# Decode query copies and two layer-norm roots moved between prompt groups, one activation block ahead of the masked maximum, the last three key pages issued behind the value copy

## The chip, the cores and the metric

The kernel runs on one core of one Trainium2 chip. The time is the device time of one execution in microseconds; for the kernel before it is 1846.37 us, the median of three runs (1846.24 to 1847.13).

## The reference

One inference step of a hybrid decoder of two layers, in float32. A prompt of 512 tokens and eight decode sequences of 8 new tokens each (behind 2048 cached tokens) go through every layer. What bears on the change is the attention half of a layer:

```python
# prompt: per group g of 4 and block t of 128 queries
s = q @ k.T * scale                     # causal, selected and window branch
p = exp(where(mask, s, -1e30) - max); p /= sum(p)
o = gate_c * p_c @ v_cmp + gate_s * p_s @ v_sel + gate_w * p_w @ v_win
# decode: per sequence, 16 gathered pages of 128 keys
kcmp = rms_norm(gelu(blocks(keys) @ w1) @ w2);  vcmp = gelu(blocks(values) @ w1) @ w2
s = q @ k_sel.T * scale                 # over the 2048 gathered keys
# beside it: a convolution branch with a layer norm over 512 channels
c = silu((y - mean) * rsqrt(var + eps) * g + b)
x = x + concat(o, c) @ w_out;  x = x + ConvFFN(rms_norm(x))
```

## The kernel before, in words

Each engine has its own instruction stream, written out by hand, and engines wait for one another on counting semaphores (`wait_ge`). Nothing is scheduled by a tool: the order in the source is the order on the engine. Per layer the stages are `glu`, `project`, `compress`, `prompt`, `decode`, `mix`, `expand`, `contract`.

**compress.** The decode keys and values are folded into blocks by two-layer perceptrons. TensorE's `hidden` (L769) writes the first layer to PSUM; VectorE's `gelu_in` (L1815 to L1817) adds the bias and forms the argument of the tanh, and counts in `cmp_in`; ScalarE's `tanhed` and VectorE's `gelu_out` (L1852) finish it. At the end of this stage VectorE runs `cmp_max` (L1869 to L1875), `key_norm`, `ln_var` and one `gelu_in`.

**prompt.** Sixteen steps v, four groups by four query blocks; the blocks are taken in the order 1, 3, 0, 2, so a score tile is 256, 512, 128 or 384 wide. In step v, TensorE does `scores(v + 2)` (L836), `weigh(v - 1)` (L873, L876) and `turn(v)` (transposes, L855; for wide blocks also `lay`, some `hidden` matmuls). VectorE does `mask(v + 1)` (mask and maximum, L1927, L1930) and `weight(v)` (L1937 to L1943). ScalarE does the exponentials (L1409) and copies the transposes out of PSUM (L1272). All scores go to the same four banks, so `scores(m)` waits for `mask(m - 1)`. Between steps VectorE does other work: `gelu_in(1)`, the decode queries copied to QB and QD (L1959, L1965), the two reciprocals of the layer norm `ln_root` (L1803), its four `ln_scale` (L1807 to L1809), and two `gelu_out`.

**decode.** Four pairs p of sequences. A pair begins with `ks_in` (L914): TensorE waits until all 32 key pages of the pair, 16 for either sequence, have landed (64 KB each), and then makes the scores (L922). The pages of the first sequence are issued by SyncE, those of the second by ScalarE, in four portions between its own work in the pair before: pages 0 to 3, 4 to 9, 10 to 12 and 13 to 15. The last lines of TensorE in a pair are `weigh` (L1040), `values_second` (L709), `keys_T` (L756), some `hidden` or output matmuls, and a transpose of the pair's output (L1075), which waits for VectorE (L2068). ScalarE takes the result of `values_second` with `values_kept(bb)` (L1272, a count in `vct_kept`), that of `keys_T` with `keys_kept(bb)`, and then copies the transposed output (`s_kept`); TensorE waits for both counts in the next pair.

```python
pe.wait_ge(*count("ks_in", 512))                    # L914
```

Of the kernel before, what the change touches and what calls it, by code (L numbers as in the profile page):

```python
# [150 lines left out]
def build(nc, I, O):  # L151
    ctx = ExitStack()
    with ctx:
# [432 lines left out]
        def _(pe):  # L586
# [232 lines left out]
            def prompt(l):  # L819
                laid = [0]  # L820

                def lay(steps):
                    job, b, n, c, bank = late[0]
                    hidden(l, job, b, n, js=range(laid[0], laid[0] + steps), bank=bank, taken=6)
                    laid[0] += steps

                def scores(v):
                    g, t = STEPS[v]
                    if v:
                        pe.wait_ge(*count("masked"))  # L830
                    n = (t + 1) * P
                    hp = [slice(HD * h, HD * (h + 1)) for h in range(2)]
                    q = [QT[hp[h], g, t * P:(t + 1) * P] for h in range(2)]
                    for e in range(2):
                        for h in range(2):
                            ins = mm(ps[:, 2 * e + h, 0:n], q[h], KT[hp[h], e, 0:n], start=True, stop=True)  # L836
                    ins.then_inc(sh["sc_made"], 1)

                def next_bank():
                    seen_of["pt_kept"] += 1  # L840
                    if seen_of["pt_kept"] > 2:
                        pe.wait_ge(sh["pt_kept"], seen_of["pt_kept"] - 2)
                    return 7 - seen_of["pt_kept"] % 2

                def turn(v):
                    t, pb = STEPS[v][1], PB[v % 3]
                    pe.wait_ge(*count("p_ready"))
                    for h in range(2):
                        if v == 0 and h == 1:
                            pe.wait_ge(*count("ct_kept", 2))  # L850
                        tiles = [(e, k) for e in range(2) for k in range(t + 1)]
                        for i in range(0, len(tiles), 4):
                            bank = next_bank()
                            for j, (e, k) in enumerate(tiles[i:i + 4]):
                                ins = tr(ps[:, bank, j * P:(j + 1) * P], pb[2 * h + e][:, k * P:(k + 1) * P], ident[:, :])  # L855
                            ins.then_inc(sh["pt_made"], 1)
                        if t >= 2 and h == 0:
                            lay(1 if v in (1, 13, 15) else 2)

                def weigh(v):  # L860
                    g, t = STEPS[v]
                    if v >= 13:
                        lay(1)
                    pe.wait_ge(sh["pt_kept"], seen_of["pt_kept"])
                    if v:
                        pe.wait_ge(*count("o_kept"))
                    out = [ps[HD * h:HD * (h + 1), 5, 0:P] for h in range(2)]
                    for e in range(2):
                        for k in range(t + 1):
                            j = e * (t + 1) + k  # L870
                            for h in range(2):
                                c = KVB + (3 + 2 * e) * P + HD * h
                                mm(out[h], Z[:, k, c:c + HD], PT[2 * h + j // 4][:, j % 4, :], start=j == 0, stop=False)  # L873
                    for h in range(2):
                        r = 32 * (2 * (g % 2) + h)
                        ins = mm(out[h], Vc[4][r:r + NCP, HD * h:HD * (h + 1)], CT8[r:r + NCP, 2 * t + g // 2, :], start=False, stop=True)  # L876
                    ins.then_inc(sh["o_made"], 1)

                pe.wait_ge(*count("cs_max"))
                pe.wait_ge(sh["var_made"], 6 * l + 4)  # L880
                scores(0)
                pe.wait_ge(sh["cmp_in"], 16 * l + 5)
                hidden(l, 2, 3, 1, js=range(8), bank=4)
                scores(1)
                hidden(l, 2, 3, 1, js=range(8, 16), bank=4)
                pe.wait_ge(sh["vct_kept"], NJOB * l + 3)
                cmp_turned()
                pe.wait_ge(sh["kct_kept"], NJOB * l + 3)
                scores(2)
                pe.wait_ge(sh["cmp_in"], 16 * l + 6)  # L890
                turn(0)
                for v in range(1, 16):
                    if v < 14:
                        scores(v + 2)
                    weigh(v - 1)
                    turn(v)
                weigh(15)
                pe.wait_ge(*count("masked"))
                pe.wait_ge(*count("o_kept"))
# [367 lines left out]
        def _(act):  # L1267
# [179 lines left out]
            def decode(l):  # L1447
                for p in range(NPR):
# [14 lines left out]
                    def fetch_keys(gs):  # L1463
                        for g in gs:
                            act.dma_start(ksT[1][:, P * g:P * (g + 1)],  # L1465
                                          I["ksT"][l, ds(page[g], 1)].rearrange("a p e -> (a p) e")).then_inc(sh["ks_in"], 16)
# [36 lines left out]
                    if more:  # L1503
                        ba, bb = JOBS[p][0][0], JOBS[p][1][0]
                        keys_squared(NCS)
                        values_kept(NCS, Vc[ba % 4], 2)
                        tanhed(tanh[1 if p < 2 else 2], NCS)
                        fetch_keys(range(10, 13))
                        keys_kept(NCS, KcT[ba % 4])
                        fetch_keys(range(13, 16))  # L1510
                        keys_squared(NCS)
                        values_kept(NCS, Vc[bb % 4], 3)
                        keys_kept(NCS, KcT[bb % 4])
                    act.wait_ge(*count("ot_made"))
                    for h in range(2):
# [104 lines left out]
        def _(dve):  # L1620
# [268 lines left out]
            def compress(l):  # L1889
                dve.wait_ge(*count("posb_kept"))  # L1890
                gelu_in(0, NCS, 2)
                taps(3, 10, 18)
                dve.wait_ge(*count("posb_kept"))
                gelu_in(1, NCS, 2)
                gelu_out(0, NCS, 2)
                gelu_out(1, NCS, 2)
                taps(3, 18, 26)
                gelu_in(0, NCM, 0, 5)
                key_means(NCS)
                taps(3, 26, 30)  # L1900
                key_norm(NCS)
                gelu_out(0, NCM, 0)
                taps(3, 30, CW)
                gelu_in(1, NCM, 0, 7)
                channel_sums()
                key_means(NCP)
                gelu_out(1, NCM, 0)
                key_norm(NCP)
                ln_centre()
                key_means(NCS)  # L1910
                cmp_max()
                key_norm(NCS)
                ln_var()
                gelu_in(0, NCS, 0)

            def prompt(l):

# [27 lines left out]

                if l:
                    dve.wait_ge(sh["causal_in"], 16 * l)
                mask(0)
                cmp_weight()
                mask(1)  # L1950
                weight(0)
                gelu_in(1, NCS, 0, 4)
                if l:
                    dve.wait_ge(sh["s_kept"], l * NPR)
                dve.wait_ge(*count("tr_kept", 10))
                for h in range(2):
                    hp = slice(HD * h, HD * (h + 1))
                    for g in range(G):
                        ins = dve.tensor_copy(QB[hp, :, 32 * h + 8 * g:32 * h + 8 * g + 8],  # L1959
                                              QT[hp, g, SEQ:NT].rearrange("p (b i) -> p b i", b=DB))  # L1960
                step(ins)
                for h in range(2):
                    src = QB[HD * h:HD * (h + 1), :, 32 * h:32 * (h + 1)]
                    for r in range(2):
                        ins = dve.tensor_copy(QD[HD * r:HD * (r + 1), :, 32 * h:32 * (h + 1)], src)  # L1965
                ins.then_inc(sh["qb_made"], 1)
                for v in range(1, 16):
                    if v < 15:
                        mask(v + 1)
                    weight(v)  # L1970
                    if v in (1, 4):
                        ln_root(v // 4)
                    if v == 6:
                        gelu_out(0, NCS, 0)
                        gelu_out(1, NCS, 0)
                    if v in (5, 8, 9, 12):
                        ln_scale((5, 8, 9, 12).index(v))
                count("pt_made", sum(BANKS[t] for g, t in STEPS[13:]))
                weight_sums_of(1)
                dve.wait_ge(sh["uc_out"], 16 * (l + 1))  # L1980
# [381 lines left out]
```

## Time and profile before

| | |
|---|---|
| median of 3 runs | 1846.37 us |
| profiled execution, own time | 1854.27 us |
| its span in the trace | 1852.5 us |
| TensorE matmuls, busy | 1816.2 us, 98% |
| VectorE busy | 1240.4 us, 67% |
| ScalarE busy | 381.3 us, 21% |
| mean granted TensorE clock | 0.994 |

The span is one profiled execution; the profile's times are microseconds from its start. PE is the matmul stream, PEld its weight loads, DVE is VectorE, ACT ScalarE, POOL GpSimd; SPq and ACTq are the sequencers of SyncE and ScalarE, which issue transfers. A row of the timeline gives start, duration, engine, line, operation, output and inputs, the count of merged instructions, and in brackets the idle time before it with what ended that. The granted clock is the share of 2.4 GHz: 1.00 is 2.4 GHz and 0.50 is 1.2 GHz.

The prompt stage of layer 0 stands at 215 to 304 us, its decode at 304 to 430; those of layer 1 at 1134 to 1223 and 1223 to 1350.

### The profile page before, as it was taken

What the parts mean: (1) busy time and instruction counts of PE and PEld (TensorE: products, weight loads), DVE (VectorE), ACT (ScalarE), POOL (GpSimd) and SP (SyncE); (2) the same over time, 40 slices, a digit from 0 to 9 for tenths busy, and PEclk for the clock granted to TensorE, in tenths of its full rate; (3) what the DMA queues carried; (4) which work ended last, traced back from release to release, by engine and by line L of the source; (5) the groups of instructions that cost most, each with busy time, mean ns of one, the idle gap of its engine ahead of it and who ended that gap; (6) DMA issues with size and microseconds to landing.
All of it is one profiled execution on the core that took longest, in us unless ns stands there. A gap on an engine that the chain in (4) does not pass through costs nothing.

```text
span 1852.5 us, 28010 instructions
## 1 busy us (share of the span) xinstructions
PE 1816.2 (98%) x10702; PEld 1406.2 (76%) x10702; DVE 1240.4 (67%) x2742; ACT 381.3 (21%) x993; POOL 118.9 (6%) x218
## 2 busy tenths in 40 slices
PE   9999999999999999999999999999999999999999
PEld 7767677787777777777777676778777777777777
DVE  5899897562676776663268997966527677676631
ACT  2013375332101000100001124853221100000000
POOL 1011400110000000000000114000100000000000
PEclk9999999999999999999999998999999999999999
DMA  7302554763122121221241044057431212222111
GB/s 279 130 1 79 169 199 144 243 210 142 46 80 80 69 91 68 78 118 63 100 153 60 1 137 130 2 179 245 172 123 49 88 68 91 68 79 111 63 63 52
DMA packets 110536, 200.15 MB, mean 108 GB/s; under 512 B 13409, under 2 KB 81266, under 8 KB 105410
## 3 DMA queue, kind: packets, MB, share of 16 engines
q1 hardware_dynamic: 91090, 162.13, 25.9%
q0 software_dynamic: 5488, 29.93, 4.6%
q10 hardware_dynamic: 13824, 6.30, 1.2%
q8 instruction: 85, 1.39, 0.3%
q14 instruction: 49, 0.40, 0.1%
HBM read 190.62 MB, written 15.94 MB: 112 GB/s over the span
## 4 chain that ended last, share of the span: by engine, by line
PE 92%; DVE 4%; issue 1%; ACT 1%; ACTq 1%; DMA 0%; POOL 0%; SPq 0%; DVEq 0%
PE ps L1106 31%; PE ps L1171 15%; PE ps L631 9%; PE ps L666 8%; PE ps L618 7%; PE ps L769 5%; PE ps L962 5%; PE ps L873 2%; PE ps L836 2%; PE ps L855 2%; PE ps L907 1%; PE ps L1040 1%; PE ps L674 1%; PE ps L922 1%; ACTq L1465 1%
## 5 line engine op out<-in xcount | busy, mean ns | idle before, releaser
L2238 DVE TENSOR_TENSOR xT<-xT,ps 128x288 f32<-128x288 f32 (+3 forms) x55 | 41.7, 758 | 153.2 <-PE ps L1171 152.6
L1106 PE MATMUL ps<-catT,rD 128*128 128x288 f32 x528 | 131.6, 406 | 0.0
L1550 ACT ACTIVATE rD<-rD 128x592 f32<-128x592 f32 x44 | 30.7, 698 | 450.0 <-DVE rD L2180 450.0
L1106 PEld LDWEIGHTS ps<-catT,rD 128*128 128x128 f32 x528 | 100.3, 190 | 27.7
L1106 PE MATMUL ps<-catT,XC 128*128 128x288 f32 x480 | 119.8, 406 | 0.4 <-DVE rD L2152 0.4
L1106 PE MATMUL ps<-rA,WR 128*128 128x288 f32 x448 | 117.8, 406 | 0.0
L1106 PEld LDWEIGHTS ps<-catT,XC 128*128 128x128 f32 x480 | 91.0, 190 | 26.2 <-issue 1.2
L1272 ACT ACTIVATE rC<-ps 128x256 f32<-128x256 f32 (+8 forms) x162 | 58.2, 387 | 232.9 <-PE ps L666 118.8
L631 PE MATMUL ps<-catT,WR 128*128 128x288 f32 x384 | 99.9, 413 | 4.4 <-issue 2.4
L1106 PEld LDWEIGHTS ps<-rA,WR 128*128 128x128 f32 x448 | 85.1, 190 | 23.5
L618 PE MATMUL ps<-rA,WR 128*128 128x288 f32 x384 | 93.4, 406 | 0.0
L1106 PE MATMUL ps<-rA,rB 128*128 128x288 f32 x336 | 88.5, 407 | 2.8 <-DVEq L2175 2.8
L631 PEld LDWEIGHTS ps<-catT,WR 128*128 128x128 f32 x384 | 71.8, 192 | 24.8 <-issue 4.8
L1691 DVE SCALAR_TENSOR_TENSOR catT<-XC,par,catT 128x512 f32<-128x512 f32 x120 | 89.6, 747 | 0.0
L618 PEld LDWEIGHTS ps<-rA,WR 128*128 128x128 f32 x384 | 73.0, 190 | 20.2
L1691 DVE SCALAR_TENSOR_TENSOR YB<-XC,par,YB 128x512 f32<-128x512 f32 x112 | 83.6, 747 | 0.0
L1106 PEld LDWEIGHTS ps<-rA,rB 128*128 128x128 f32 x336 | 63.7, 190 | 21.1 <-DVEq L2175 3.7
L666 PE MATMUL ps<-rB,rA 128*128 128x326 f32 x256 | 71.6, 437 | 0.0
L2144 DVE TENSOR_TENSOR rD<-rD,ps 128x288 f32<-128x288 f32 x42 | 19.1, 454 | 78.3 <-PE ps L1106 78.3
L666 PEld LDWEIGHTS ps<-rB,rA 128*128 128x128 f32 x256 | 48.5, 189 | 21.7
L769 PE MATMUL ps<-WR,rD 128*128 128x258 f32 (+1 forms) x256 | 59.8, 384 | 0.2
L1106 PE MATMUL ps<-catT,WR 128*128 128x288 f32 x224 | 58.9, 406 | 0.0
(405 smaller groups left out, 3527.6 us busy)
## 6 DMA issues: line engine op xcount, KB each, us to landing
WR<-in_w_up SPq DMA_DIRECT2D x56, 512.0 KB, 3.7
WR<-in_kvc SPq DMA_DIRECT2D x128, 128.0 KB
rB<-in_w_up SPq DMA_DIRECT2D x32, 512.0 KB, 4.4
rD<-in_kvc SPq DMA_DIRECT2D x96, 128.0 KB, 2.5
rD<-in_w_down SPq DMA_DIRECT2D x8, 1408.0 KB, 7.7
rB<-in_ksT SPq DMA_DIRECT2D x160, 64.0 KB
rB<-in_w_down SPq DMA_DIRECT2D x6, 1408.0 KB, 7.8
WR<-in_w_glu SPq DMA_DIRECT2D x16, 512.0 KB, 4.0
```

What stands on the lines that cost most here:

```text
L618: ins = mm(ps[:, bank + hf, 0:HN], w[:, k * P:(k + 1) * P], rhs[:, k, hf * HN:(hf + 1) * HN], start=k == 0, stop=k == K - 1)
L631: ins = mm(ps[:, bank, 0:HN], w[:, k, :], rhs[:, k, hf * HN:(hf + 1) * HN], start=k == first, stop=k == last)
L666: ins = mm(ps[0:m, 4 * (t % 2) + ch, 0:CHW], hT[:, k, t * P:t * P + m], weights(ch, k), start=k == 0, stop=k == KD - 1)
L769: ins = mm(out[:, 0:2 * nb].rearrange("p (c h) -> p c h", h=2), w1[n][:, j, :], chunks[:, j // NPAIR:j // NPAIR + nb, o:o + 2], start=j == ...
L836: ins = mm(ps[:, 2 * e + h, 0:n], q[h], KT[hp[h], e, 0:n], start=True, stop=True)
L855: ins = tr(ps[:, bank, j * P:(j + 1) * P], pb[2 * h + e][:, k * P:(k + 1) * P], ident[:, :])
L962: ins = mm(thirds(bank)[part], w, rows[:, :, o:o + 2], start=j == 0, stop=j == NPAIR - 1)
L1106: ins = mm(ps[:, bank, 0:HN], w[:, k, :], h[:, k, :], start=k == 0, stop=k == 3)
L1171: ins = mm(ps[:, bank, 0:HN], w(k), h(k), start=k == 0, stop=k == FH - 1)
L1272: return act.activation(out, in_, ACT.Copy)
L1691: ins = stt(y, xc[:, k:k + SEQ], w, y, ALU.mult, ALU.add)
L2238: step(tt(x, x, src, ALU.add))
```

## The change: what it does

Four edits, without any instruction added or taken out but one wait:

1. TensorE's wait for the sixth count of `cmp_in` ahead of `turn(0)` is gone. The first `lay`, in `turn(1)`, waits for the same count already.
2. In `compress` VectorE's `gelu_in(0)` stands ahead of `cmp_max` and not behind `ln_var`.
3. In `prompt` VectorE's `gelu_in(1)` moves from ahead of step 1 to between `mask(2)` and `weight(1)`; the query copies move to step 8; the two `ln_root` from steps 1 and 4 to 4 and 6; the four `ln_scale` from 5, 8, 9, 12 to 9, 10, 12, 13.
4. In `decode` ScalarE issues pages 13 to 15 behind `keys_squared` and `values_kept(bb)` and not ahead of them.

```diff
@@ compress and prompt, TensorE @@
                 scores(2)
-                pe.wait_ge(sh["cmp_in"], 16 * l + 6)
                 turn(0)
@@ decode, ScalarE @@
                         fetch_keys(range(10, 13))
                         keys_kept(NCS, KcT[ba % 4])
-                        fetch_keys(range(13, 16))
                         keys_squared(NCS)
                         values_kept(NCS, Vc[bb % 4], 3)
+                        fetch_keys(range(13, 16))
                         keys_kept(NCS, KcT[bb % 4])
@@ compress, VectorE @@
                 key_means(NCS)
+                gelu_in(0, NCS, 0)
                 cmp_max()
                 key_norm(NCS)
                 ln_var()
-                gelu_in(0, NCS, 0)
@@ prompt, VectorE @@
+                def queries_laid():
+                    if l:
+                        dve.wait_ge(sh["s_kept"], l * NPR)
+                    dve.wait_ge(*count("tr_kept", 10))
...
+                    ins.then_inc(sh["qb_made"], 1)
+
                 mask(0)
                 cmp_weight()
                 mask(1)
                 weight(0)
-                gelu_in(1, NCS, 0, 4)
-                if l:
-                    dve.wait_ge(sh["s_kept"], l * NPR)
-                dve.wait_ge(*count("tr_kept", 10))
...
-                ins.then_inc(sh["qb_made"], 1)
                 for v in range(1, 16):
                     if v < 15:
                         mask(v + 1)
+                    if v == 1:
+                        gelu_in(1, NCS, 0, 4)
                     weight(v)
-                    if v in (1, 4):
-                        ln_root(v // 4)
+                    if v in (4, 6):
+                        ln_root(v // 6)
+                    if v == 8:
+                        queries_laid()
                     if v == 6:
                         gelu_out(0, NCS, 0)
                         gelu_out(1, NCS, 0)
-                    if v in (5, 8, 9, 12):
-                        ln_scale((5, 8, 9, 12).index(v))
+                    if v in (9, 10, 12, 13):
+                        ln_scale((9, 10, 12, 13).index(v))
```

The body of `queries_laid` is the code that stood in line before. Line numbers of VectorE's part are one to five lower after the change.

VectorE at the start of the prompt stage, before the change: the end of `weight(0)`, then `gelu_in(1)`, the query copies, and the first instruction of `mask(2)`.

```order
L1943 TENSOR_SCALAR rA<-rA,st 128x256 x4
L1815 TENSOR_SCALAR rC<-ps,posb 128x254
L1816 SCALAR_TENSOR_TENSOR rC<-rC 128x254
L1817 SCALAR_TENSOR_TENSOR rC<-rC 128x254
L1959 COPY QB<-rC 64x8x8 x8
L1965 COPY QD<-QB 64x8x32 x4
L1927 ISA XC,st<-ps,causal 128x128
```

And the same place with the change:

```order
L1942 TENSOR_SCALAR rA<-rA,st 128x256 x4
L1926 ISA XC,st<-ps,causal 128x128
...
L1929 TENSOR_SCALAR st<-st 128x4
L1814 TENSOR_SCALAR rC<-ps,posb 128x254
L1815 SCALAR_TENSOR_TENSOR rC<-rC 128x254
L1816 SCALAR_TENSOR_TENSOR rC<-rC 128x254
L1936 TENSOR_SCALAR st<-st 128x4
```

`mask(2)` follows `weight(0)` at once, and `gelu_in(1)` stands behind it.

VectorE at the end of step 8 with the change: the end of `weight(8)`, the query copies, and the first instruction of `mask(10)`. Before, the three instructions of an `ln_scale` stood in the place of the copies.

```order
L1942 TENSOR_SCALAR XC<-XC,st 128x256 x4
L1954 COPY QB<-rC 64x8x8 x8
L1960 COPY QD<-QB 64x8x32 x4
L1926 ISA rC,st<-ps,causal 128x128
L1926 ISA st 128x1
```

ScalarE near the end of a pair in decode, before the change; a DMA row is one key page, and `kct_made` and `cmp_out` are counts by TensorE of a transpose and of a second layer.

```order
L1272 ACTIVATE rC<-ps 128x127 [waits kct_made]
L1465 ISA
L1465 DMA rB<-in_ksT 128x128
...
L1465 DMA rB<-in_ksT 128x128
L1350 ACTIVATE KN<-ps 127x128 [waits cmp_out]
L1272 ACTIVATE rC<-ps 127x128 [waits cmp_out]
```

With the change:

```order
L1271 ACTIVATE rC<-ps 128x127 [waits kct_made]
L1349 ACTIVATE KN<-ps 127x128 [waits cmp_out]
L1271 ACTIVATE rC<-ps 127x128 [waits cmp_out]
L1464 ISA
L1464 DMA rB<-in_ksT 128x128
L1464 ISA
L1464 DMA rB<-in_ksT 128x128
L1464 ISA
L1464 DMA rB<-in_ksT 128x128
```

The three pages now stand behind the second `cmp_out`, which TensorE counts after its last weighted sums of the pair.

## Rows read from the trace of the kernel before

**Rows 1.** The page, part 1: TensorE's busy time and share.

```profile
PE 1816.2 (98%) x10702; PEld 1406.2 (76%) x10702; DVE 1240.4 (67%) x2742; ACT 381.3 (21%) x993; POOL 118.9 (6%) x218
```

**Rows 2.** Timeline, TensorE, layer 0 prompt: scores and weighted sums, steps 1 and 5.

```profile
231.69 2.12 PE L836 MATMUL ps<-rC 64*128 64x384 f32 x8 [1.70 <-DVE st L1930]
233.74 1.98 PE L873 MATMUL ps<-rA,rC 128*64 128x128 f32 x16
...
252.00 1.56 PE L836 MATMUL ps<-rC 64*128 64x384 f32 x8 [0.59 <-DVE st L1930]
253.49 1.09 PE L873 MATMUL ps<-rA,rC 128*64 128x128 f32 x16
```

**Rows 3.** Timeline, VectorE, same stretch: gelu_in(1), the query copies, ln_root(0).

```profile
226.92 0.48 DVE L1815 TENSOR_SCALAR rC<-ps,posb 128x254 f32<-128x254 f32 x1
...
228.23 1.01 DVE L1959 COPY QB<-rC 64x64 f32<-64x64 f32 x8
229.27 1.19 DVE L1965 COPY QD<-QB 64x256 f32<-64x256 f32 x4
...
233.74 1.94 DVE L1803 RECIPROCAL rA<-rA 128x288 f32<-128x288 f32 x1
```

**Rows 4.** Timeline, TensorE, layer 1 prompt: scores of step 1.

```profile
1150.04 2.29 PE L836 MATMUL ps<-rC 64*128 64x384 f32 x8 [1.70 <-DVE st L1930]
```

**Rows 5.** Windows: stretch, length, busy PE PEld DVE ACT POOL, granted clock, DMA share, GB/s.

```profile
229.10:232.50 3.40, 1.47 (x10) 0.97 (x12) 3.15 (x19) 2.09 (x8) 1.70 (x3) 1.00 1.45 431
232.50:235.90 3.40, 3.40 (x24) 1.99 (x22) 3.37 (x6) 0.82 (x5) 0.00 (x0) 0.51 0.81 325
362.30:365.70 3.40, 2.05 (x59) 1.63 (x58) 1.34 (x6) 0.28 (x1) 0.70 (x1) 1.00 1.04 313
365.70:369.10 3.40, 3.40 (x32) 1.75 (x39) 1.12 (x5) 1.43 (x6) 0.00 (x0) 0.50 0.59 192
```

**Rows 6.** Timeline, steps 8 and 11 of layer 0: last mask instruction, TensorE's next scores.

```profile
270.23 0.17 DVE L1930 TENSOR_SCALAR st<-st 128x4 f32<-128x4 f32 x1
270.45 1.56 PE L836 MATMUL ps<-rC 64*128 64x384 f32 x8
278.94 0.17 DVE L1930 TENSOR_SCALAR st<-st 128x4 f32<-128x4 f32 x1
280.10 1.99 PE L836 MATMUL ps<-rC 64*128 64x512 f32 x8
```

**Rows 7.** Timeline, ScalarE, end of pair 0, layer 0: page issues, keys squared, values_kept(bb).

```profile
330.41 1.82 ACTq L1465 DMA_DIRECT2D rB<-in_ksT  x3
332.28 0.28 ACT L1350 ACTIVATE KN<-ps 127x128 f32<-127x128 f32 x1 [1.72 <-PE ps L709]
333.85 0.28 ACT L1272 ACTIVATE rC<-ps 127x128 f32<-127x128 f32 x1 [1.29 <-PE ps L709]
```

**Rows 8.** Timeline, TensorE, end of pair 0: keys_T, and the next pair's scores.

```profile
334.57 0.33 PE L756 MATMUL ps<-ident,KN 127*128 127x127 f32 x1 [0.75 <-DVE KN L1863]
...
335.63 1.95 PE L922 MATMUL ps<-rB,QD 64*32 64x512 f32 x32
```

**Rows 9.** Timeline, pair 2 of layer 0, and a window (columns as in rows 5).

```profile
396.03 1.49 ACTq L1465 DMA_DIRECT2D rB<-in_ksT  x3
399.47 0.28 ACT L1272 ACTIVATE rC<-ps 127x128 f32<-127x128 f32 x1 [1.63 <-PE ps L709]
400.91 1.95 PE L922 MATMUL ps<-rB,QD 64*32 64x512 f32 x32
398.50:399.00 0.50, 0.50 (x16) 0.41 (x11) 0.00 (x0) 0.00 (x0) 0.50 (x1) 1.00 0.05 11
```

**Rows 10.** Timeline, pair 1: SyncE's transfers in layer 0, the rest in layer 1.

```profile
358.96 10.94 SPq L359 DMA_DIRECT2D rD<-in_kvc  x16
1280.12 1.35 ACTq L1465 DMA_DIRECT2D rB<-in_ksT  x3
1284.19 0.45 ACT L1272 ACTIVATE rC<-ps 127x128 f32<-127x128 f32 x2 [2.39 <-PE ps L709]
1285.09 0.18 PEld L922 LDWEIGHTS ps<-rB,QD 64*32 64x32 f32 x16 [0.31 <-DMA rB<-in_ksT]
```

More of the change, by code:

```diff
@@ L1947, in prompt @@
                     dve.wait_ge(sh["causal_in"], 16 * l)
+                def queries_laid():
+                    if l:
+                        dve.wait_ge(sh["s_kept"], l * NPR)
+                    dve.wait_ge(*count("tr_kept", 10))
+                    for h in range(2):
+                        hp = slice(HD * h, HD * (h + 1))
+                        for g in range(G):
+                            ins = dve.tensor_copy(QB[hp, :, 32 * h + 8 * g:32 * h + 8 * g + 8],
+                                                  QT[hp, g, SEQ:NT].rearrange("p (b i) -> p b i", b=DB))
+                    step(ins)
+                    for h in range(2):
+                        src = QB[HD * h:HD * (h + 1), :, 32 * h:32 * (h + 1)]
+                        for r in range(2):
+                            ins = dve.tensor_copy(QD[HD * r:HD * (r + 1), :, 32 * h:32 * (h + 1)], src)
+                    ins.then_inc(sh["qb_made"], 1)
                 mask(0)
@@ L1951, in prompt @@
                 weight(0)
-                gelu_in(1, NCS, 0, 4)
-                if l:
-                    dve.wait_ge(sh["s_kept"], l * NPR)
-                dve.wait_ge(*count("tr_kept", 10))
[L1956 to L1965, printed above, removed]
-                ins.then_inc(sh["qb_made"], 1)
                 for v in range(1, 16):
```

## Prediction

> **What bounds the kernel now.** I read the page first: TensorE is busy for 98% of the span [rows 1]. So an edit gains only where it shortens a wait of TensorE or raises its clock, and costs only where it makes TensorE wait or lowers its clock. I then read TensorE's timeline for its idle time in the two stages that the change touches, the windows for the clock granted there, and the timelines of VectorE and ScalarE for what stood ahead of the instruction that ended each wait.
>
> In the prompt stage one wait stands out. The scores of step 1 start after 1.70 us of idle time, ended by VectorE's last mask instruction [rows 2]; in layer 1 it is 1.70 us again [rows 4]. VectorE had reached that mask late: ahead of it stood gelu_in(1), from 226.92, and the query copies, from 228.23 to 230.46 [rows 3]. None of them is needed by these scores.
>
> Right behind this wait the granted clock falls: TensorE is busy for 1.47 of 3.40 us, and in the next 3.40 us it has 0.51 of the full clock, that is its lower level, 1.2 GHz [rows 5]. The scores take 2.12 us where the same shape takes 1.56, and the weighted sums 1.98 where they take 1.09 [rows 2].
>
> In decode I looked at how a pair hands over to the next. ScalarE issues the last three key pages of pair 0 at 330.41; the copy behind which the change puts them starts at 333.85 [rows 7]. TensorE starts the next pair at 335.63 [rows 8], and it may not start before the last page is there. For pair 1 of layer 1 it even waits for the page already, 0.31 us, though the issue was at 1280.12 and the start at 1285.09 [rows 10]. That is the place which decides.
>
> **The change part by part.**
>
> *The missing wait of TensorE and gelu_in(1) behind mask(2).* With gelu_in(1) and the copies gone from its way, VectorE has mask(2) ready about 2.7 us sooner, before TensorE's transposes end. The 1.70 us go in each layer. The transposes themselves gain nothing from the missing wait: their second half waits for a copy of ScalarE. Since TensorE is then busy through this stretch, I expect the lower clock to go with the wait: (2.12 - 1.56) + (1.98 - 1.09) = 1.45 us, about 1.6 with the shorter pieces behind. The bounds are 0, if the clock falls all the same, and 1.7, half of 3.4 us. Together -3.3 us per layer.
>
> *What the moved VectorE work then costs.* A piece of work between steps is free only as far as VectorE is ahead of TensorE. At step 8 the mask ends at 270.40 and TensorE takes up its scores at 270.45 [rows 6]: there is no room, and the ln_scale that stood there (1.35 us) is replaced by the copies, 1.01 + 1.19 us plus gaps, 2.27 [rows 3]. That makes a new wait of 0.9 - 0.1 = 0.8 us. At step 10 an ln_scale comes in where the mask had 280.10 - 279.11 = 1.0 us to spare [rows 6]: 1.35 - 1.0, about 0.4. At step 6 a root of 1.94 us [rows 3] comes in and an ln_scale goes at step 5: between 0 and 0.6, I take 0.3. Step 4 keeps a root as before, with its wait of 0.59 [rows 2]. Step 13 and the missing root of step 1 lie beside idle time of VectorE. Given back: 1.5 us per layer. Query copies are needed only by decode, so step 8 is early enough; SyncE waits for them behind the end of the prompt stage, so nothing in its queue gets later.
>
> *gelu_in(0) ahead of cmp_max.* It moves into idle time of VectorE, while the scores which were its cover keep running; TensorE's next matmuls wait 0.1 us less. Prompt stage: -3.3 + 1.5 - 0.1 = -1.9 us per layer, **-3.8 us** in all.
>
> *The last three pages.* ScalarE works in order, so they are issued 0.1 us after values_kept(bb) starts. What lies between the first issue and the last landing? In pair 2 of layer 0 the issue is at 396.03 and the transfers have ended in the window that begins at 398.50, some 2.9 us later [rows 9]: this is the lower bound. The upper bound is from pair 1: at most 4.97 us in layer 1 [rows 10], with SyncE's 16 transfers of 10.94 us running beside it [rows 10]. So for pair 0 of layer 0: 333.85 + 0.1 + 2.9 = 336.9 against 335.63, a loss of 1.3 us. Pair 2: 399.47 + 3.0 = 402.5 against 400.91, 1.6 us. Layer 1 has the same pattern: 1.45 and 1.7. For pair 1 the lower bound gives 1284.19 + 3.0 - 1285.09 = 2.1 us and the upper one 4.2; in layer 0 it is 1.5 to 4.6. I take 4.8 us for the two: SyncE's queue is behind there, so when TensorE comes later, SyncE's transfers end sooner beside it. Sum of the six: 1.3 + 1.6 + 1.45 + 1.7 + 4.8 = **+10.9 us**, bounds 9.7 and 14.9.
>
> There is a gain in this edit, but it is swallowed. The squaring at 332.28 came after the issues [rows 7]; without them keys_T would lose its wait of 0.75 us [rows 8]. TensorE only comes to the page wait sooner. What stands behind the three issues on ScalarE gets late too: keys_kept(bb) and the copy of the pair's output, which TensorE needs for the second half of the key scores. At 336.8 it is there just before the pages, so it is hidden by them, and would cost 0.4 us per pair if they were not late.
>
> *The clock in decode.* TensorE stands still for about 2 us at five of the six hand-overs at least, and the work before it is made of small matmuls. In layer 0 a stretch of this kind, 2.05 us busy out of 3.40, is already followed by 3.4 us at 0.50 [rows 5]. I reckon with such a fall at five of the six, each at the 1.6 us of the prompt stage, less the one that is there now: 5 x 1.6 - 1.6 = **+6.4 us**. The bounds are -1.6 (none, and the present one gone) and 8.6 (six, at 1.7).
>
> **The sum** is -3.8 + 10.9 + 6.4 = +13.5 us. The durations are from an execution of 1854.27 us (span 1852.5), which is 7.9 us over the median; I carry the difference over: 1846.37 + 13.5 = 1859.9 us.
>
> **The rivals.**
>
> *Waits without the clock.* The pages are late as above, but the clock holds or falls no more often than now: -3.8 + 10.9 = +7.1, 1853.5 us. For it: pair 0 has idle pieces in decode now without a fall at the hand-over. Against it: those are below 1 us.
>
> *Every hand-over falls to the low clock, and pair 1 waits its upper bound.* After each late page the first 3.4 us run at half speed: -3.8 + 14.9 + 8.0 = +19.1, 1865.5 us. For it: the fall at 365.70 came with 2.05 us of work in the stretch before [rows 5], and the new gaps leave less. Against it: SyncE's queue drains sooner. The Trainium skill, "TensorE: Matmul & The Clock Gate", section "HAM oscillation — how this bites in real kernels", describes exactly this: a kernel that waits for a transfer ahead of each tile loses the clock ahead of each tile, and pays every time. By that rule this rival would be the result; the trace agrees as far as the fall behind the 1.70 us wait of both prompt stages goes.
>
> *The pages come in time.* If ScalarE's queue ran ahead of its waiting copy, or three pages landed within 1.1 us (the time from values_second to the next pair without the keys_T wait), only the prompt gain would remain, less 0.3 us per pair for the output copy: -3.8 + 1.8 = -2, 1844.4 us, not slower. It decides at a loss of about 0.6 us per pair. Against it: the three issues alone take 1.35 to 1.82 us [rows 7, 10], and they are seen behind a waiting copy, never ahead of it.
>
> *The change doesn't do what it says in the prompt.* The clock falls there all the same, or the new waits of steps 6, 8 and 10 take everything: -3.8 becomes 0, 1863.7 us.
>
> **How the numbers follow.** Forecast 0.48; waits without the clock 0.17; every hand-over and the upper bound 0.17; no prompt gain 0.11; pages in time 0.04; something in my reading of decode that I don't see, on either side, 0.03. The likeliest case gives 1859.9. The range takes in the first three and the fourth with their bounds: 1852 to 1867. A measurement of this kernel can tell about 0.2%, 3.7 us, from no change. Slower by more than that holds in all cases but the pages in time and part of the unseen: 0.93. Same 0.04, faster 0.03.
>
> **What the new profile would show.** Right in the prompt: the scores of step 1 start without idle time, full clock behind them, a wait of some 0.8 us at the scores after step 8. Right in decode: PEld L922 of pairs 1 to 3 waits for DMA rB<-in_ksT, 2 us and more, the three ACTq rows start 0.1 us after values_kept(bb), and stretches of 0.50 clock follow. I am wrong if the L922 rows show no DMA wait, or if TensorE's later waits in a pair shrink by as much as the page wait adds.

## The result and the profile after

The changed kernel takes 1876.86 us (median of 4 runs, 1871.82 to 1881.51) against 1846.30 us before, measured beside it: ratio 1.015, 95% interval 1.0128 to 1.0171 (the quotient of the two medians, 1.0166, lies inside it). The forecast was 1859.9 us, with a range of 1852 to 1867. The direction was right and the size was not: +30.6 us, where +13.5 was expected. The time lies above the range and above the slowest rival, 1865.5 us.

The profiled execution took 1876.91 us with a span of 1874.8 us, so it stands for the median. The one before took 7.9 us more than its median. Part of that can be seen: in its compression stage of layer 1 TensorE ran 10.2 us at the lower clock, which the profile after does not have. The stage took 62.07 us there and 57.29 us after, 4.78 us that no edit made; four of the experiments below show the same piece in layer 0.

The page of the changed kernel, part 1 [rows 1]:

```profile
PE 1814.8 (97%) x10702; PEld 1399.3 (75%) x10702; DVE 1240.5 (66%) x2742; ACT 379.6 (20%) x993; POOL 118.3 (6%) x218
```

TensorE's timeline: layer 0's prompt stage, steps 1, 5, 7, 9 and 11, then four of the six hand-overs in decode [rows 2, 8 to 10]:

```profile
229.03 0.66 PE L855 MATMUL ps<-ident,rA 128*128 128x128 f32 x4 [1.00 <-ACT rB L1271]
229.62 1.56 PE L836 MATMUL ps<-rC 64*128 64x384 f32 x8
231.12 1.09 PE L873 MATMUL ps<-rA,rC 128*64 128x128 f32 x16
...
248.35 1.56 PE L836 MATMUL ps<-rC 64*128 64x384 f32 x8 [0.59 <-DVE st L1929]
258.27 1.99 PE L836 MATMUL ps<-rC 64*128 64x512 f32 x8 [0.29 <-DVE st L1929]
268.07 1.56 PE L836 MATMUL ps<-rC 64*128 64x384 f32 x8 [0.87 <-DVE st L1929]
278.05 1.99 PE L836 MATMUL ps<-rC 64*128 64x512 f32 x8 [0.34 <-DVE st L1929]
...
335.18 3.67 PE L921 MATMUL ps<-rB,QD 64*32 64x512 f32 x32 [3.50 <-DMA rB<-in_ksT]
373.43 3.67 PE L921 MATMUL ps<-rB,QD 64*32 64x512 f32 x32 [4.31 <-DMA rB<-in_ksT]
415.74 3.56 PE L921 MATMUL ps<-rB,QD 64*32 64x512 f32 x32 [8.23 <-DMA rB<-in_ksT]
...
1342.44 3.67 PE L921 MATMUL ps<-rB,QD 64*32 64x512 f32 x32 [5.79 <-DMA rB<-in_ksT]
```

The prompt stage came out as forecast. The scores of step 1 start without idle time and run at full clock (1.56 and 1.09 us, where they took 2.12 and 1.98). The new waits behind steps 6, 8 and 10 are 0.29, 0.87 and 0.34 us; I had written 0.3, 0.8 and 0.4. (The scores at 270.45 in [rows 6], headed step 8 there, are TensorE's step 9; the mask ahead of them follows VectorE's step 8.) From the stage's first scores to the first scores of decode it is 87.16 us where it was 89.08, and 87.17 for 89.09 in layer 1: -1.9 us per layer.

The loss is in decode. The group of the first key scores, by form, says how much TensorE waits for the last pages: 30.0 us, all at six hand-overs.

```profile
L921 PE MATMUL ps<-rB,QD 64*32 64x512 f32 x256 | 25.6, 932 | 30.9 <-DMA rB<-in_ksT 30.0 <-issue 0.8
```

The windows over the two decode stages split the loss. Columns as in [rows 5]; first the kernel before, then the changed one. Each stretch runs from the first key scores to the first product of the expansion, so the short `mix` stage is in it too.

```profile
304.74:489.88 185.14, 180.36 (x1905) 147.76 (x1906) 100.11 (x303) 50.95 (x128) 12.33 (x16) 0.99 0.56 185
1223.12:1411.43 188.31, 180.69 (x1906) 148.36 (x1906) 100.28 (x303) 50.92 (x128) 12.35 (x16) 0.99 0.55 177
```

```profile
302.68:506.64 203.96, 184.87 (x1905) 148.03 (x1906) 100.38 (x303) 50.55 (x128) 12.30 (x16) 0.93 0.51 168
1233.16:1433.75 200.59, 183.52 (x1906) 147.83 (x1907) 100.50 (x303) 50.55 (x128) 12.32 (x16) 0.96 0.50 166
```

Length less busy time of PE is its idle time. Both stages together grow from 373.45 to 404.55 us, by 31.1. Idle time grows from 12.4 to 36.2, by 23.8; busy time grows from 361.1 to 368.4, by 7.3, with the same instructions, so that is the lower clock (0.93 and 0.96 granted in place of 0.99). My terms for the two were +10.9 and +6.4. The account closes: 31.1 - 3.8 (prompt) - 4.8 (the piece that was chance) = 22.5 us, and the spans differ by 22.3.

So the clock's term was about right, and the pages' term was less than half of what came. Why are the pages that late? At the hand-over after pair 2 of layer 0, ScalarE and GpSimd of the changed kernel show this:

```profile
406.29 1.00 POOL L509 DMA_INDIRECT rC<-in_cache_v_slc,idx  x1 [0.61 <-PE ps L1039]
407.59 0.95 POOL L509 DMA_INDIRECT rC<-in_cache_v_slc,idx  x1 [0.30 <-issue]
...
406.63 0.28 ACT L1271 ACTIVATE rC<-ps 127x128 f32<-127x128 f32 x1 [2.24 <-PE ps L709]
406.76 1.80 ACTq L1464 DMA_DIRECT2D rB<-in_ksT  x3
```

and the DMA view of 406.7 to 416 us has these queues and issues:

```profile
q0 software_dynamic: 288, 2.10, 60.1%
q10 hardware_dynamic: 432, 0.20, 7.3%
...
rC<-in_cache_v_slc,idx POOLq DMA_INDIRECT x2, 7.0
```

From the first issue to the scores it is 415.74 - 406.76 = 9.0 us, for 0.2 MB. (In a second profile of the same kernel, which stands under "The clock's share" below, this hand-over took 6.5 us with a wait of 5.70, so 9.0 is the worst case seen and not the rule.) The same instruction that ends a pair's weighted sums (pv_done) releases GpSimd's two gathers for the pair after, 2.1 MB. Before the change the last pages were issued 3 us ahead of that point; now they are issued 0.5 us behind it. The trace of before had the row that I did not read, at 399.31, where values_kept(bb) starts at 399.47 [rows 9]:

```profile
399.31 1.00 POOL L509 DMA_INDIRECT rC<-in_cache_v_slc,idx  x1 [0.17 <-issue]
```

At pair 1 the gathers wait for something else, but there pv_done releases SyncE's window and new rows for pair 3. The changed kernel shows them beside the pages, which are issued at 367.85 and take 5.6 us from there to the scores: SyncE's timeline, and the DMA view of 366 to 374 us with the size and the time from issue to landing:

```profile
367.12 0.39 SPq L364 DMA_DIRECT2D rC<-in_kwT  x1
367.56 1.00 SPq L365 DMA_DIRECT2D rC<-in_state_v_win  x1
```

```profile
rC<-in_kwT SPq DMA_DIRECT2D x1, 512.0 KB, 3.5
rC<-in_state_v_win SPq DMA_DIRECT2D x1, 512.0 KB, 5.7
```

At pair 0 pv_done releases no transfer at once. That gave the theory for the experiments. **A:** pages 13 to 15 are late because they enter the DMA engines together with what pv_done releases. **B**, the rival: they are late by issue time and latency alone, and the traces of before were too few to show how long that is. A second question is how much of the loss is the clock, and a third whether the prompt edits have any part in the decode loss.

### The profile page after: what moved, and what is told of

The parts are those of the page before. It is cut to its first block, busy times and chain, and to the rows that moved or that the text cites. A ratio compares the mean times of both kernels' runs of the same rounds, so it can differ in the third digit from the quotient of the medians.

```text
span 1874.8 us, 28011 instructions
## 1 busy us (share of the span) xinstructions
PE 1814.8 (97%) x10702; PEld 1399.3 (75%) x10702; DVE 1240.5 (66%) x2742; ACT 379.6 (20%) x993; POOL 118.3 (6%) x218
## 4 chain that ended last, share of the span: by engine, by line
PE 89%; DVE 6%; DMA 2%; issue 1%; ACT 1%; ACTq 1%; DVEq 0%
PE ps L1105 30%; PE ps L1170 15%; PE ps L631 8%; PE ps L666 7%; PE ps L618 7%; PE ps L769 5%; PE ps L961 4%; PE ps L1039 2%; PE ps L836 1%; DMA rB<-in_ksT 1%; PE ps L921 1%; PE ps L873 1%; PE ps L906 1%; PE ps L855 1%; PE ps L674 1%
```

## Experiments

Ratios are to the kernel before, run on the same chip, with 95% intervals. Its medians there lie between 1847.9 and 1850.8 us, so ratios are compared and not medians.

### The pages back, and the pages alone

The changed kernel with the issues where they were:

```
-                        keys_squared(NCS)
-                        values_kept(NCS, Vc[bb % 4], 3)
                         fetch_keys(range(13, 16))
+                        keys_squared(NCS)
+                        values_kept(NCS, Vc[bb % 4], 3)
```

> The changed kernel with the last three key pages issued where they were before, ahead of keys_squared(bb); the prompt-stage edits stay. Theory A (the whole loss is in the decode hand-overs, the prompt edits gain 1.9 us per layer): no wait of PEld L921 for rB<-in_ksT over 0.4 us, and 3.8 us faster than before, 1842.5 us. Rival (the prompt edits disturb decode too, through the later query layout or a shifted clock): a time between 1846 and 1877.

Measured: 1845.11 us, ratio 0.998 (0.9967 to 0.9992), that is -3.7 us (0.002 x 1851). TensorE waits 1.3 us for pages in all, at one hand-over (pair 1 of layer 1, where the kernel before waited 0.31); theory A had no wait over 0.4, so on that point it missed. The two decode stretches take 371.66 us together, where the kernel before took 373.45.

The kernel before with the opposite edit and nothing else:

> The kernel before with nothing changed but the three issues moved behind values_kept(bb). Theory A: the six hand-overs cost 30.5 + 3.8 = about 34 us by themselves, 1880.5 us, with some 30 us of waiting for the pages as in the changed kernel. Rival B (the landing takes the 2.9 to 5 us that the trace of before shows, and the prompt edits made the rest of the loss): 17 us by my forecast's own terms, 1863.6 us.

Measured: 1875.42 us, ratio 1.0134 (1.0119 to 1.0149), +25 us, with 24.0 us of page waits. Theory A of that run had said 34 us; the waits were 6 us shorter than in the changed kernel. But 17 us, all that my forecast's terms give, is outside the interval too (1.0092). Together: the prompt edits gain 3.7 us and lose nothing in decode that these runs can show; the page edit makes the whole loss. The two do not add exactly (+25 - 3.7 is 21, the changed kernel has +28 by its ratio). Against the changed kernel's first profile the difference in the waits is all in layer 0. At pair 1 this run waits 2.42 us, and the changed kernel 4.31 and 4.13 in its two profiles. Here SyncE issues its window at 372.97, 1.9 us behind the pages (371.12); in the changed kernel it does so at 367.12, 0.7 us ahead of them. At pair 2 it is 5.17 against 8.23 and 5.70, so two profiles of one kernel differ there by as much.

### The collision taken away

SyncE and GpSimd wait until the next pair's pages have landed:

```
                     if p == 1:
+                        sp.wait_ge(sh["ks_in"], 512 * (NPR * l + 3))
                         fetch_window(l, 3)
...
                             pool.wait_ge(sh["imp_kept"], NPR * l + p + 2)
+                        else:
+                            pool.wait_ge(sh["ks_in"], 512 * (NPR * l + 4))
                         gather_values(l, p + 1)
```

> The changed kernel, with two groups of transfers held back until the next pair's key pages have landed: SyncE's window and new rows for pair 3 (released by pv_done of pair 1) and GpSimd's two gathers for pair 3 (released by pv_done of pair 2). Theory A (in pairs 1 and 2 the three pages share the DMA engines with 1.0 MB and 2.1 MB that pv_done releases at the same moment): the waits of the pairs 1 and 2 fall from 4.3, 8.2, 5.7 and 5.8 us to about the 2.5 to 3.5 us of the two pairs 0, some 10 to 12 us less in all, 1865 to 1867 us. Rival B (issue time and the latency of one transfer are all): the waits stay, 1877 us.

Measured: 1861.57 us, ratio 1.0051 (1.0036 to 1.0066). The group of this run, its decode windows, and TensorE's timeline at the three hand-overs of layer 0:

```profile
L924 PE MATMUL ps<-rB,QD 64*32 64x512 f32 x256 | 23.7, 868 | 15.9 <-DMA rB<-in_ksT 15.1 <-issue 0.8
```

```profile
307.83:503.86 196.03, 186.05 (x1906) 149.30 (x1907) 100.42 (x303) 50.59 (x128) 12.30 (x16) 0.95 0.53 174
1230.40:1423.33 192.93, 182.20 (x1906) 147.78 (x1907) 100.57 (x303) 50.55 (x128) 12.32 (x16) 0.97 0.52 173
```

```profile
340.19 3.49 PE L924 MATMUL ps<-rB,QD 64*32 64x512 f32 x32 [3.38 <-DMA rB<-in_ksT]
375.46 3.67 PE L924 MATMUL ps<-rB,QD 64*32 64x512 f32 x32 [1.36 <-DMA rB<-in_ksT]
412.55 3.67 PE L924 MATMUL ps<-rB,QD 64*32 64x512 f32 x32 [2.63 <-DMA rB<-in_ksT]
```

The waits behind pairs 1 and 2 fall from 4.31, 8.23, 5.72 and 5.79 us to 1.36, 2.63, 3.16 and 2.08. The two behind pairs 0, where nothing was held back, stay: 3.50 and 2.48 against 3.38 and 2.50. That is A, and half of the page waits is the collision. With it gone, the pages take 2.8 to 4.1 us from the first issue to the scores (the issues at 336.06, 372.57 and 409.16 for the three rows above): the 1.3 to 2.4 us in which ScalarE issues three, and 1.5 to 2 us behind. That is the size that I had forecast for the changed kernel, and the idle time says the same: 388.96 - 368.25 = 20.7 us, 8.3 more than before, where my term was 10.9 with 9.7 as its lower bound. The time fell by more than A said: from a ratio of 1.015 to 1.0051 is some 18 us, where I had written 10 to 12, and the profiled execution, 1866.51 us, was the slowest of the six, so its waits may be on the long side.

### One page in place of three

```
-                        keys_squared(NCS)
+                        fetch_keys(range(13, 15))
+                        keys_squared(NCS)
                         values_kept(NCS, Vc[bb % 4], 3)
-                        fetch_keys(range(13, 16))
+                        fetch_keys(range(15, 16))
```

> The changed kernel with only the last page behind values_kept(bb) and pages 13 and 14 ahead of keys_squared(bb). Theory A (a page that is issued at the same moment as 1.0 or 2.1 MB of other transfers is late however small it is): the waits of pairs 2 stay above 4 us, and more than half of the loss stays, 1862 to 1870 us. Rival B (the length of the train of issues, 1.3 to 2.3 us, is what is late): each wait shrinks by the two issues, about 1.1 us, and by nothing in the pairs that a delayed values_kept(bb) makes later; 1868 to 1872 us with the same waits in pairs 1 and 2 relative to each other. Rival C (only three pages together are too much): no wait over 1 us, 1846 us.

Measured: 1853.38 us, ratio 1.0016 (1.0004 to 1.0029), and 11.2 us of page waits: 1.22, 2.12, 2.42, 1.12, 3.36 and 0.94. All three expectations missed. A was wrong in its number (above 4 us at pairs 2), for a single page gets through with 1.7 to 4.1 us from issue to scores. B was wrong too, since the waits fell by much more than two issues. The profile is from the fastest execution of the twelve, 1847.59 us, so the waits of a typical one may be longer than these. Beside the gathers (pairs 2) the one page took 3.3 and 1.7 us from issue to scores, where three took 9.0 and 6.5; at pairs 0, with neither gathers nor window, it took 2.1 and 1.9. The longest wait of this run stands at pair 1 of layer 1:

```profile
1276.91 0.34 ACTq L1464 DMA_DIRECT2D rB<-in_ksT  x1
1281.02 3.55 PE L921 MATMUL ps<-rB,QD 64*32 64x512 f32 x32 [3.36 <-DMA rB<-in_ksT]
```

SyncE issues its window only at 1281.72, behind these scores. What ran beside this page were the pieces of 128 KB that SyncE issues ahead of the window (L359, twelve of them between 1274.1 and 1281.7). So pv_done's transfers are not the only ones that make a page late.

The delay beside the gathers grows with the number of pages. The sizes fit an explanation that I argue and have not shown. In the window above, 288 packets of the gathers carry 2.10 MB, 7.3 KB each, and 432 packets of the key pages carry 0.20 MB, 0.46 KB each. A small packet that takes turns with a large one would wait for it every time, and three pages have three times as many turns as one. In the second profile of the changed kernel, from the issue to the scores (405.8 to 412.5 us), 1.80 MB of the gathers went by in 236 packets while the 0.20 MB of the pages went by in 432, so the two did not share by bytes. But one page is also issued sooner: its issue takes 0.34 us and three take 1.3 to 1.8 us, and when the scores began after it only 77 packets of the gathers had moved at pair 2 of layer 0. This run does not tell the two apart. The Trainium skill, "DMA: Bandwidth & Descriptors", section "Queues, rings and completion order", gives such turns as the rule: each DMA engine goes round the queues that have work for it, one packet at a time. This case's times agree (9.0 us for 0.2 MB beside 2.1 MB), though no run here looked at the order of single packets.

### The clock's share

Sixteen products of the identity with itself, into a bank that the next scores write over, ahead of TensorE's wait:

```
+                    for k in range(16 if p else 0):
+                        mm(ps[:, 0, 0:P], ident[:, :], ident[:, :], start=True, stop=True)
                     pe.wait_ge(*count("ks_in", 512))
```

> The changed kernel once more, on the same chip as the three below, as their common reference: 1.015 of the time before, some 1875 to 1878 us. If chips differ it is this run, and not the first, from which the differences below are taken.

> The changed kernel with 16 products of the identity with itself (128x128, into bank 0, which the next scores write over) ahead of the wait for the pages at the start of pairs 1 to 3: about 1.8 us of TensorE's work that fits into each of the six waits of 2.5 us and more. Theory A (part of the loss is the lower clock that follows a stretch with idle time): the pages land when they did, the idle time shrinks to 30 - 11 = 19 us, stretches at half clock get fewer or shorter, and the time falls by up to the 8 us that the clock costs, 1869 to 1873 us. Rival B (the waits alone are the loss, the clock costs nothing net since what follows the scores waits for VectorE anyway): the same time, 1876 us.

Measured on one chip: the changed kernel 1875.76 us, ratio 1.015 (1.0122 to 1.0179); with the products 1862.47 us, ratio 1.0076 (1.0047 to 1.0106). The decode windows and the group of the first run:

```profile
302.56:503.60 201.04, 185.85 (x1906) 148.94 (x1906) 100.47 (x303) 50.55 (x128) 12.30 (x16) 0.93 0.51 170
1230.12:1432.20 202.08, 185.24 (x1906) 148.44 (x1906) 100.46 (x303) 50.57 (x128) 12.32 (x16) 0.94 0.50 165
```

```profile
L921 PE MATMUL ps<-rB,QD 64*32 64x512 f32 x256 | 25.9, 942 | 28.4 <-DMA rB<-in_ksT 27.5 <-issue 0.8
```

and of the one with the products (L914), whose stage is the same:

```profile
302.92:495.29 192.37, 188.24 (x2001) 157.44 (x2002) 100.43 (x303) 50.56 (x128) 12.30 (x16) 1.00 0.54 178
1221.84:1415.14 193.30, 188.09 (x2001) 157.41 (x2002) 100.35 (x303) 50.57 (x128) 12.32 (x16) 1.00 0.53 172
```

```profile
L914 PE MATMUL ps<-ident 128*128 128x128 f32 x192 | 22.4, 276 | 0.0
L923 PE MATMUL ps<-rB,QD 64*32 64x512 f32 x256 | 15.6, 595 | 6.5 <-DMA rB<-in_ksT 5.6 <-issue 0.8
```

Useless work makes the kernel 13 us faster. TensorE is held up for as long as before, 22.4 + 5.6 = 28.0 us against 27.5, but the clock stays at 1.00 through both stages, and the scores take 1.95 us each time and not 3.67. The real work shrinks from 371.1 to 376.3 - 22.4 = 353.9 us: 17 us of the changed kernel's decode are the lower clock. These are two single executions, 1875.37 and 1858.31 us, and the second is the fastest of its six (the others have a mean clock of 0.994 to 1.000); between the medians it is 13.3 us. My expectation had two mistakes. The products took 3.74 us per hand-over and not 1.8, about 1 us more than the waits behind the two pairs 0 had room for; and the gain was above the 8 us that I thought the clock could cost. The kernel before has such time as well, by the same subtraction 361.1 - 353.9 = 7 us, so the change adds 7 to 10 us of it.

### The pages earlier

Where should they stand, then? Two versions on top of the changed kernel. The first puts the issues between keys_squared(bb) and values_kept(bb), 2.2 us earlier:

> The changed kernel with the three issues one step earlier, between keys_squared(bb) and values_kept(bb), so about 2.2 us earlier, and ahead of pv_done's transfers. Theory A: the waits shrink by more than the 2.2 us in the pairs 1 and 2, since the pages are then ahead of what they collide with: about 1 us is left at each of six hand-overs, and with half of the clock falls left some 10 us over the version with the pages back, about 1852 us. Rival B (no contention): each wait is shorter by 2.2 us and no more, 1877 - 13 = 1864 us.

Measured: 1844.40 us, ratio 0.9964 (0.9951 to 0.9977), with 5.2 us of page waits and no keys_T wait. That is better than A's 1852, and A's 1 us at each hand-over is not what came: layer 0 has no wait, layer 1 has 1.49, 2.96 and 0.78. The 2.96 are at pair 1 again. The pages are issued at 1274.59, the scores start at 1280.82, and SyncE issues its window only at 1281.15; between 1274.1 and 1281.1 it issues eleven of its 128 KB pieces (L359). Ahead of pv_done three pages are nearly in time elsewhere, and what is left of the wait is mostly paid by the keys_T wait that is gone (3.3 us in the run with the pages back).

The second moves both groups of three one place up:

```
                         keys_squared(NCS)
+                        fetch_keys(range(10, 13))
                         values_kept(NCS, Vc[ba % 4], 2)
                         tanhed(tanh[1 if p < 2 else 2], NCS)
-                        fetch_keys(range(10, 13))
+                        fetch_keys(range(13, 16))
                         keys_kept(NCS, KcT[ba % 4])
                         keys_squared(NCS)
                         values_kept(NCS, Vc[bb % 4], 3)
-                        fetch_keys(range(13, 16))
```

> The changed kernel with ScalarE's issues one place earlier than before, not later: pages 10 to 12 between keys_squared(ba) and values_kept(ba), in ScalarE's idle time of 1.7 us there, and pages 13 to 15 where 10 to 12 stood. Theory A: the last pages land 2 to 3 us before TensorE wants them, no wait at the hand-over is left, and keys_T loses its wait of 0.3 to 2.0 us as well; with the prompt edits 6 to 8 us faster than before, ratio 0.996 to 0.997. Rival (the three issues before values_kept(ba) delay that copy and what waits for it, or the earlier pages only move a wait): the same as the version with the pages back, ratio 0.998.

Measured: 1842.28 us, ratio 0.9967 (0.9951 to 0.9983), 0.3 us of page waits. The pair that took 30.89 us takes 28.83. The same move in the kernel before, without the prompt edits:

> The kernel before with nothing but ScalarE's issues one place earlier. Theory A (the two parts of the gain are independent): the decode pairs are shorter by what they are in the version that has both, 3.5 us of keys_T waits and a little of the clock, and the prompt gain of 3.8 us is missing: ratio 0.998 to 0.999. Rival B (the gain of the version with both was the prompt's alone): the time of before, ratio 1.000.

Measured: 1845.66 us, ratio 0.9987 (0.9976 to 0.9998). That is A's ratio, and with the 0.998 of the prompt edits alone it gives the 0.9967 of both, so the two parts are independent as far as these intervals reach; B's 1.000 lies just outside.

Last, the query copies, on top of the version with both groups one place up. The copies into QB (`queries_laid`) go to where VectorE of the changed kernel is idle for 1.38 us, and those into QD, now a function of their own (`queries_doubled`), behind the weights of step 15:

```
-                    if v == 8:
+                    if v == 14:
                         queries_laid()
...
+                queries_doubled()
                 count("pt_made", sum(BANKS[t] for g, t in STEPS[13:]))
```

> The version with ScalarE's issues one place earlier (ratio 0.9967 to before), with the query copies in two pieces and later: the eight copies into QB behind the weights of step 14, where VectorE is idle for 1.38 us, and the four into QD behind those of step 15. Theory A (the wait of 0.87 us at the scores after step 8 is made by these copies alone): that wait goes in both layers, no other grows, and the prompt stage is 0.8 to 0.9 us shorter per layer, 85.4 us from its start to that of decode's first scores in place of 87.17; the time falls by 1.7 us, ratio about 0.9958. Rival B (VectorE is behind all the way there, and a wait of the same length comes back at the transposes of step 15 or at the start of decode): 87.2 us per layer and the same time.

Measured: 1841.42 us, ratio 0.9963 (0.9949 to 0.9977). The prompt stage is 86.40 us where it was 87.18, and 86.39 in layer 1, so 0.8 us per layer, as A had it. (The 85.4 us in A was a slip of mine: 87.2 less 0.8 to 0.9 is 86.3.) TensorE's timeline at the scores that waited 0.87 us:

```profile
266.27 1.09 PE L855 MATMUL ps<-ident,XC 128*128 128x128 f32 x8
267.30 1.56 PE L836 MATMUL ps<-rC 64*128 64x384 f32 x8
```

The wait is gone, and no other has grown. The step of 1.6 us in the time is too small for these intervals. This version has the lowest ratio of all, but its interval overlaps with those of the two versions on top of the changed kernel above (0.9964 and 0.9967). All three are 6 to 7 us faster than the kernel before, and which of them is best stays open.

## Why the prediction was right and wrong

**The prompt stage, right, by an argument with a gap.** -3.8 us was forecast; the trace has -1.92 and -1.93, the pages-back run -3.7. Each new wait was within 0.1 us. The gap is in what the clock was worth. In layer 1 of the run with the pages edit alone, the fall behind step 1 happens not to come. By my working that should have made the stage 1.45 us shorter; it was 88.56 against 89.09, 0.5 us. TensorE just met VectorE earlier, at the next scores:

```profile
1160.81 1.56 PE L836 MATMUL ps<-rC 64*128 64x384 f32 x8 [1.81 <-DVE st L1930]
1162.30 1.09 PE L873 MATMUL ps<-rA,rC 128*64 128x128 f32 x16
1167.09 1.13 PE L836 MATMUL ps<-rC 64*128 64x256 f32 x8 [0.92 <-DVE st L1930]
```

So in the kernel before, the clock alone would give back 0.5 us of its 1.45. It can give all of it only where VectorE's queue is also shorter there, which the same edit does; that it does give all of it is inferred from the total of -1.92 us.

**The last pages, wrong.** This is the step that failed: "*What lies between the first issue and the last landing? In pair 2 of layer 0 the issue is at 396.03 and the transfers have ended ... some 2.9 us later: this is the lower bound.*" The 2.9 us were measured 3 us ahead of pv_done, with nothing else under way: the DMA view of the kernel before from 396 to 399 us has the 432 packets of the three pages and no others. They were used for an issue 0.5 us behind pv_done. I weighed SyncE's queue for pair 1 only, and GpSimd's not at all. From issue to scores it came to 4.3 and 3.2 us at pairs 0, 5.6 and 6.4 at pairs 1 (upper bound: 4.97), 9.0 and 6.6 at pairs 2 (taken: 2.9). As idle time the term was +23.8 us, not +10.9. With pv_done's transfers held back it is +8.3.

**SyncE behind pair 1, wrong in its sign.** "*when TensorE comes later, SyncE's transfers end sooner beside it.*" They do, and SyncE then goes on at once to the window of pair 3: it issued that at 369.95 in the kernel before, behind the start of the scores (367.25), and at 367.12 now, where the pages are.

**The gain of keys_T, right but small.** Its waits in the kernel before were 0.75, 0.41, 0.57 and 0.29 us at four of the six hand-overs and none at the pairs 1; all are gone. As forecast, TensorE only came to the page wait sooner.

**The clock in decode, right in size, in part by luck.** +6.4 was forecast, +7.3 is what busy time grew by (+10.0 in the second profile of the same kernel). All six hand-overs are followed by the lower clock, not five. I took off 1.6 us for the one fall that I had seen in the kernel before; by the run with the products it has about 7 us of such time in decode, and the changed kernel 14 to 17. Both ends were too low, and the difference came out. The rival built on the rule of the Trainium skill ("TensorE: Matmul & The Clock Gate", "HAM oscillation — how this bites in real kernels") had every hand-over fall, and that part of it was the better forecast; its time fell short because it had 14.9 us for the pages. The traces bear the rule out only in part. In the run with the pages edit alone TensorE waits 2.55 us ahead of the scores at 341.41, and they take 1.95 us at a granted clock of 1.00; with one page in place of three it is the same behind a wait of 2.42 us (scores at 402.30). And in the kernel before the clock falls at 365.70 [rows 5] with no page wait at all. So a wait of this length makes a fall likely, and does not settle it.

**The range** ended at 1867 because four of its six page terms were made from rows of transfers that had the DMA engines to themselves, and the upper bound of the other two, 4.97 us, had SyncE's pieces beside it but not the window. Nothing in it stood for a collision with what pv_done releases.

**Still open:** why the hand-over after pair 2 of layer 0 takes 9.0 us in one profile of the changed kernel and 6.5 in the other; whether it is the number of small packets or the time of the last issue that makes three pages so much later than one; how much of the waits at pairs 1 is SyncE's window and how much the pieces ahead of it; and what decides whether the clock falls behind a wait of about 2.5 us.

## What to carry to other kernels

A transfer's time from issue to landing holds only for the moment where it was measured. Before moving an issue, list what every other queue sends at its new place, above all what the same semaphore releases and what is still under way from before, and take the landing time from a row with that traffic beside it. And when TensorE must wait, count the wait and the slower clock behind it apart: the windows give both, as idle time and as growth of busy time with the same instructions.

## What the runs showed that I had not expected

- 0.2 MB in 432 packets of 0.46 KB took 9.0 us beside 2.1 MB in 288 packets of 7.3 KB (6.5 us in a second profile), and three pages take 2.8 to 4.1 us with pv_done's transfers held back. A small transfer was hurt by a large one out of all proportion to its size.
- 22.4 us of products whose result nobody reads made the kernel 13.3 us faster (1875.76 to 1862.47); in the profiled execution the granted clock stayed at 1.00 through decode.
- Three issues of ScalarE took from 1.33 to 3.04 us (at 327.58 in the pages-back run), so the place of an issue costs its engine an amount that no single row tells.
- A stretch of 10.2 us at the lower clock in the compression stage, worth 4.8 us, came in layer 1, in layer 0 or not at all from one profiled execution to the next, with the same code there.
